# Two buffers for the rearranged and turned tiles of the sample compression, the bias table loaded behind the gathers, and more projection in the recurrence's first interval

## What is computed

```python
def compress(rows, pe, w1, w2):
    b, length = rows.shape[:2]
    n_chunks = length // CMP_STRIDE
    r = CMP_BLOCK // CMP_STRIDE
    n_cmp = n_chunks - r + 1
    ch = rows[:, :n_chunks * CMP_STRIDE].reshape(b, n_chunks, CMP_STRIDE, N_KV_HEADS, HEAD_DIM)
    blocks = jnp.concatenate([ch[:, i:i + n_cmp] for i in range(r)], axis=2)
    blocks = blocks + pe[:, None, :]
    flat = jnp.transpose(blocks, (0, 1, 3, 2, 4)).reshape(b, n_cmp, N_KV_HEADS, CMP_BLOCK * HEAD_DIM)
    return jax.nn.gelu(flat @ w1) @ w2

def layer_front(h, lw):
    z = rmsnorm(h, lw['attn_norm']) @ lw['w_in']
    ...
```

## Time and profile before

| | |
|---|---|
| median of 3 runs | 1233.44 us (1232.53 to 1235.86) |
| the profiled execution | 1235.16 us |
| its span | 1233.3 us |
| PE busy, share of the span | 93% |
| DVE, ACT, POOL | 41%, 33%, 34% |
| mean granted clock of PE | 0.961 |

### The profile page before, as it was taken

The page is one execution under the profiler, slowest core; times in us unless marked ns, Lnnn a source line. Parts: engine busy times, 40 slices in busy tenths (PEclk is TensorE's granted clock), DMA queues, the critical chain, the costliest instruction groups (busy, mean ns, idle before and its releaser), DMA issues.

```text
span 1233.3 us, 19665 instructions
## 1 busy us (share of the span) xinstructions
PE 1150.4 (93%) x8351; PEld 992.8 (80%) x8351; DVE 503.9 (41%) x939; ACT 403.1 (33%) x728; POOL 421.4 (34%) x247
## 2 busy tenths in 40 slices
PE   4998999979798999889799999999999999999996
PEld 4996888868444457455579999999999999999996
DVE  4848787666000001667547533323233230011354
ACT  5422332332332213557542224232322221222413
POOL 1266688583200003000204432343434344434230
PEclk9988999989789999889999999999999999999999
DMA  7434274542583107000518222222333322323311
GB/s 202 131 71 125 57 225 139 165 139 87 110 147 121 48 1 267 24 2 2 172 47 276 86 86 69 86 86 87 88 89 92 92 82 78 93 78 99 108 30 73
DMA packets 162803, 125.08 MB, mean 101 GB/s; under 512 B 20699, under 2 KB 151227, under 8 KB 161180
## 3 DMA queue, kind: packets, MB, share of 16 engines
q1 hardware_dynamic: 156956, 102.59, 30.3%
q0 software_dynamic: 3456, 16.78, 4.1%
q10 hardware_dynamic: 2304, 4.46, 0.9%
HBM read 112.27 MB, written 15.69 MB: 104 GB/s over the span
## 4 chain that ended last, share of the span: by engine, by line
PE 84%; DVE 6%; ACT 4%; issue 2%; DMA 1%; POOL 1%; SPq 1%; ACTq 0%; DVEq 0%; POOLq 0%
PE pair L1694 15%; PE pair L1696 15%; PE pair L1695 15%; PE pair L1906 9%; PE pair L1658 4%; PE pair L1660 4%; PE pair L1659 4%; PE pair L1701 2%; PE pair L2088 2%; DVE arena L1181 2%; PE pair L1876 1%; PE pair L2058 1%; PE pair L1865 1%; PE pair L1890 1%; PE pair L2068 1%
## 5 line engine op out<-in xcount | busy, mean ns | idle before, releaser
L708 POOL TENSOR_TENSOR ring_r<-ring,ring_r 128x1024 fp32r<-128x1024 f32 (+2 forms) x123 | 289.2, 2359 | 502.8 <-ACT ring_r L807 502.1
L1694 PE MATMUL pair<-zT_r,ring_r 128*128 128x272 f32 x928 | 270.6, 292 | 0.0
L1696 PE MATMUL pair<-zT_r,ring_r 128*128 128x272 f32 x928 | 268.6, 289 | 0.0
L1695 PE MATMUL pair<-uT_r,ring_r 128*128 128x272 f32 x832 | 239.5, 288 | 0.0
L1694 PEld LDWEIGHTS pair<-zT_r,ring_r 128*128 128x128 f32 x928 | 174.7, 188 | 0.4
L1696 PEld LDWEIGHTS pair<-zT_r,ring_r 128*128 128x128 f32 x928 | 174.6, 188 | 0.0
L807 ACT ACTIVATE ring_r<-ring 128x1024 fp32r<-128x1024 f32 (+2 forms) x123 | 124.8, 1031 | 122.4 <-PE pair L1696 94.3
L1695 PEld LDWEIGHTS pair<-uT_r,ring_r 128*128 128x128 f32 x832 | 156.9, 189 | 0.3
L1658 PE MATMUL pair<-arena_r,ring_r 128*128 128x272 f32 (+1 forms) x496 | 147.9, 298 | 7.8 <-ACT arena L881 6.9
L1694 PE MATMUL pair<-arena_r,ring_r 128*128 128x272 f32 x512 | 148.7, 290 | 0.9 <-issue 0.9
L1696 PE MATMUL pair<-arena_r,ring_r 128*128 128x272 f32 x512 | 148.2, 289 | 0.0
(11 more groups left out here) (299 smaller groups left out, 1642.8 us busy)
## 6 DMA issues: line engine op xcount, KB each, us to landing
ring<-in_w_in SPq DMA_DIRECT2D x26, 512.0 KB, 5.0
ring<-in_w_ffn_gate SPq DMA_DIRECT2D x22, 512.0 KB, 3.8
ring<-in_w_ffn_up SPq DMA_DIRECT2D x22, 512.0 KB, 3.8
ring<-in_w_ffn_down SPq DMA_DIRECT2D x16, 512.0 KB, 4.0
mg_spill<-arena ACTq DMA_DIRECT2D x16, 272.0 KB, 4.3
arena<-mg_spill SPq DMA_DIRECT2D x8, 544.0 KB, 8.3
arena<-in_cmp_w_v SPq DMA_DIRECT2D x4, 1024.0 KB, 6.0
ring<-in_w_o SPq DMA_DIRECT2D x8, 512.0 KB, 4.1
```

The source lines that it names most:

```text
L708: eng.tensor_tensor(ring_r[:, n % RING, 0:slab_size(n)], ring[:, n % RING, 0:slab_size(n)], hi, ALU.subtract).then_inc(S["slab_split"], 1)
L1694: eng.matmul(out, w_hi, x_hi(k)[:, cols], start=n == 0, stop=False)
L1695: eng.matmul(out, w_hi, x_lo(k)[:, cols], start=False, stop=False)
L1696: ins = eng.matmul(out, w_lo, x_hi(k)[:, cols], start=False, stop=n == len(steps) - 1)
```

## The change

Five things change; the arithmetic stays.

1. `fill` takes 36 steps in interval 0 and 25 or 26 in the others, instead of 26 or 27.
2. POOL's gather 0 moves from behind rotation 13 to behind rotation 11, and ACT's `raw_copy(0)` from g = 12 to g = 13. Splits 33 to 35 move from ahead of gather 2 to behind gather 3; ACT's copies for them (`high_after` of the last three groups) move from the projection's end to behind `raw_copy(2)`.
3. `raw2` and `XT` are there twice, the second pieces in the arena where the projection's and the recurrence's tiles have been; `glu_sig` moves to make room, and a memset on DVE that now lies over the second XT moves behind `cs_done`.
4. PE issues the turns of the next batch among the hidden matmuls of this one, one bank (4 transposes) after every 4 matmuls, and the second product of a batch after the first 4 matmuls of the next.
5. The bias table is loaded after the second half of the value network's `w1`, which gets a semaphore of its own, `w1_rest_in`.

```diff
-        XT = uT[:, :, :].rearrange("p a b -> p (a b)")[:, 0:4096].rearrange("p (q k n) -> p q k n", q=8, k=KV)
+        XT = [x.rearrange("p (q k n) -> p q k n", q=8, k=KV) for x in (uT[:, :, :].rearrange("p a b -> p (a b)")[:, 0:4096], ar(7304, 4096))]
-        raw2 = ar(22528, 2048)
+        raw2 = [ar(22528, 2048), ar(11528, 2048)]
...
             half_w1("cmp_w1_v", 0)
             eng.wait_ge(S["hid_done"], 8)
-            half_w1("cmp_w1_v", 1)
+            half_w1("cmp_w1_v", 1, "w1_rest_in")
+            for p0 in range(0, P, SHIFTS):
+                bias_table(p0)
...
-                if j in (13, 15):
-                    if j == 13:
+                if j in (11, 15):
+                    if j == 11:
                         eng.wait_ge(S["idx_ready"], 2)
                         eng.wait_ge(S["kv_out"], 16 * 12)
-                    gather_cmp(j // 2 - 6)
-            for n in range(33, 36):
-                split(n)
+                    gather_cmp(j // 15)
             for n in range(2, 8):
                 gather_cmp(n)
+                if n == 3:
+                    for m in range(33, 36):
+                        split(m)
...
             def raw_copy(n):
                 eng.wait_ge(S["raw_in"], 16 * (n + 1))
-                if n:
-                    eng.wait_ge(S["raw_turned"], 4 * n)
+                if n >= 2:
+                    eng.wait_ge(S["raw_turned"], 4 * (n - 1))
...
-                if g == 12:
+                if g == 13:
                     raw_copy(0)
...
-                high_after(name)
+                if g < 13:
+                    high_after(name)
...
+            for q in range(8):
+                if q == 4:
+                    raw_copy(1)
+                turn_out()
+            raw_copy(2)
+            for g in range(13, 2 * KC):
+                high_after(("mg%d" % (g % 2), g // 2))
+            raw_copy(3)
+            for batch in range(4):
+                if batch:
+                    second_out(batch - 1)
+                for q in range(8):
+                    if q == 6:
+                        hidden_out(batch, 0)
+                    if batch < 3:
+                        turn_out()
+                    if batch < 2 and q == 3:
+                        raw_copy(2 * batch + 4)
+                hidden_out(batch, 1)
+                if batch < 2:
+                    raw_copy(2 * batch + 5)
             second_out(3)
...
-            eng.memset(ce[:, :, CB_P:32], 0.0)
             eng.wait_ge(S["toep_in"], 16 * KV * P // SHIFTS)
             mx, sm = csum[:, 0:32], csum[:, 32:64]
             eng.wait_ge(S["cs_done"], 1)
+            eng.memset(ce[:, :, CB_P:32], 0.0)
...
-                fill(26 + j % 4 // 2)
+                fill(36 if j == 0 else 25 + j % 4 // 2)
...
             for batch in range(4):
-                for half in range(2):
-                    for h in range(2):
-                        hidden(h, half, batch)
-                if batch < 3:
-                    turns()
-                    turns()
-                second(batch // 2)
+                steps = hidden_steps(batch)
+                for q in range(8):
+                    for _ in itertools.islice(steps, 4):
+                        pass
+                    if q == 0 and batch:
+                        second((batch - 1) // 2, 4 + 2 * batch)
+                    if batch < 3:
+                        turn_rows()
+            second(1, 12)
```

More of the change, by code:

```diff
@@ L602, in _, with bias_table @@
             eng.wait_ge(S["line_out"], 16)
-            for p0 in range(0, P, SHIFTS):
+            def bias_table(p0):
                 for k in range(KV):
@@ L1894, in hidden @@
-            def hidden(h, half, batch):
-                nonlocal hid
-                if half == 0:
-                    if batch:
-                        eng.wait_ge(S["hid_taken"], 4 + 2 * (batch - 1) + h + 1)
-                    if h == 0:
-                        eng.wait_ge(S["turn_copied"], 8 * (batch + 1))
-                        eng.wait_ge(S["w1_in"], 64 if batch < 2 else 96)
-                out = bank(h)[:, 0:504].rearrange("p (k b c) -> p k b c", k=KV, c=CB_S)
-                for q in range(8):
-                    rhs = XT[:, q, :, :].rearrange("p k (b c) -> p k b c", c=64)[:, :, :, half:half + CB_S]
-                    ins = eng.matmul(out, w1[:, 8 * half + q, h * P:(h + 1) * P], rhs, start=half == 0 and q == 0, stop=half == 1 and q == 7)
-                if half:
-                    ins.then_inc(S["hid_done"], 1)
-                    hid += 1
-                elif h and batch == 1:
-                    ins.then_inc(S["half_done"], 1)
@@ L1913, in second @@
-            def second(kv):
+                n, q = turn // 4, turn % 4
+                ckv, ph = q // 2, q % 2
+                if q == 0:
+                    eng.wait_ge(S["raw_copied"], n + 1)
+                if turn >= 2:
+                    eng.wait_ge(S["turn_copied"], turn - 1)
+                for c in range(4):
+                    col = (4 * ph + c) * 256 + ckv * P
+                    ins = eng.transpose(bank(2 + turn % 2)[:, c * P:(c + 1) * P], raw2[n % 2][:, col:col + P], ident)
@@ new lines, in turn_rows, with hidden_steps @@
+                ins.then_inc(S["raw_turned"], 1)
+                turn += 1
+            def hidden_steps(batch):
+                for half in range(2):
+                    for h in range(2):
+                        if half == 0:
+                            if batch:
+                                eng.wait_ge(S["hid_taken"], 4 + 2 * (batch - 1) + h + 1)
+                            if h == 0:
+                                eng.wait_ge(S["turn_copied"], 8 * (batch + 1))
+                                eng.wait_ge(S["w1_in"], 64 if batch < 2 else 80)
+                        elif h == 0 and batch == 2:
+                            eng.wait_ge(S["w1_rest_in"], 16)
+                        out = bank(h)[:, 0:504].rearrange("p (k b c) -> p k b c", k=KV, c=CB_S)
+                        for q in range(8):
+                            rhs = XT[batch % 2][:, q, :, :].rearrange("p k (b c) -> p k b c", c=64)[:, :, :, half:half + CB_S]
+                            ins = eng.matmul(out, w1[:, 8 * half + q, h * P:(h + 1) * P], rhs, start=half == 0 and q == 0, stop=half == 1 and q == 7)
+                            if q == 7 and half:
+                                ins.then_inc(S["hid_done"], 1)
+                            elif q == 7 and h and batch == 1:
+                                ins.then_inc(S["half_done"], 1)
+                            yield q
```

67 lines of the change are left out of this document (24 added, 43 removed).

## The result

The changed kernel takes **1196.32 us** in the median of 4 runs (1193.35 to 1198.02) against 1233.9 beside it: a ratio of **0.969**, 95% interval 0.9671 to 0.9709. The profiled execution took 1197.42 us with a span of 1195.6. The forecast was 1202, its range 1196 to 1211: the direction and the mechanism held, the gain came out some 6 us larger than the 31.3 forecast.

> The changed kernel as it is, beside the next ones on the same chip: 1196 (1193 to 1199), 0.969 of before.

The account below looks back on a forecast made before the run. PE, busy 93% of the span, was taken as the bound, so time is won only where it waits or runs at lower clock. 8.3 + 8.0 + 7.1 + 8.0 − 0.1 = 31.3 off 1233.44 gave 1202 us, range 1196 to 1211.

Parts of the forecast that it names:

- Part 1: Recurrence, interval 0: 36 steps instead of 26 remove PE's wait on DVE and half clock at x_pair(2); net 8.3 us.
- Part 2: Recurrence, mg 12: earlier gather 0 and later raw_copy(0) remove PE's 6.9 us wait on ACT and half clock; net 8.0.
- Part 3: Projection's end to first hidden matmul: ACT's copies no longer stand behind late slab loads; 16.20 becomes 9.1, net 7.1 us.
- a case that I had given to a rival: Clock falls in small gaps left in part 3 and between batches, one to three times: 1205 to 1211 us; chance 0.13.
- Part 4: The four batches: turns among hidden matmuls and double buffers cut 139.5 us to 131.5; net 8.0.
- The rest: Bias table's move, w1_in split and glu_sig cost nothing; the memset moved behind cs_done costs 0.1 us.
- POOL bound one interval only: Rival in the recurrence: POOL's splits and DVE hold PE in each interval, half of parts 1 and 2 lost: 1210; chance 0.05.
- The buffers do not overlap: Rival in parts 3 and 4: every tile still waits for gather and copy, little won there: about 1217 us; chance 0.03.
- The rival on the slower side: Interleaved transposes hold PE at its lower clock through batches 0 to 2: 1297 us; chance 0.04.

Follow-up runs that it names:

- e2: The kernel before with only gather_cmp(0) two rotations earlier on POOL and raw_copy(0) at g = 13: 1231.85 us, ratio 0.9985.
- e5: The changed kernel with the bias table's 16 transfers back at their old place on SP's queue: 1210.4 us.
- e4: The changed kernel with a batch's eight turns in one piece behind its 32 hidden matmuls, both double buffers kept: 1206.24 us.
- e6: The changed kernel with every turn issued twice, or eight times, over the same bank: batches of 136.8 us and 199.7 us.
- e1: The kernel before with only the projection steps per interval changed (36, then 25 and 26 in turn): 1224.07 us, ratio 0.9918.

## Why the prediction's mechanism held, and which step of its sum failed

**Part 1** held: no wait at x_pair(2), no stretch at 0.50, x_pair(4) at 137.95 (forecast near 138), one new wait of 1.2 on POOL at slab 13 (forecast 1.0). **Part 2** held in kind and missed in two sizes. The new wait at x_pair(14) was 1.5, not 2.5 (DVE's recurrence 12 started at 241.93, 27.8 behind x_pair(10), where I had 28.2, and PE came a little later than I had it). And the half clock behind the old wait of 6.9 cost more than x_pair(14) and y_sums. PE, in order of time in the kernel before:

```profile
273.31 0.60 PE L1658 MATMUL pair<-arena_r,ring_r 128*128 128x272 f32 x1 [6.86 <-ACT arena L881]
273.71 0.43 PE L1659 MATMUL pair<-uT_r,ring_r 128*128 128x272 f32 x1
...
282.64 0.42 PE L1659 MATMUL pair<-uT_r,ring_r 128*128 128x272 f32 x1
282.87 0.32 PE L1660 MATMUL pair<-arena_r,ring_r 128*128 128x272 f32 x1
283.02 0.29 PE L1658 MATMUL pair<-arena_r,ring_r 128*128 128x272 f32 x1
```

The steps ahead of x_pair(14) and behind y_sums ran slow too, from 273.31 to 282.9: 9.6 us, a loss of 4.8 where I counted 3.6. With a wait of 0.6 on an earlier output of ACT that went away as well, the terms are 5.6 + 3.7 − 1.2 + 6.9 + 4.8 − 1.5 + 0.6 = 18.9, against 18.55 measured and 16.3 forecast. The prediction counted the six steps that part 1 brings into part 2's sum, but not that part 2 hangs on them: e2 shows that without them 4.47 of the 6.9 come back.

**Part 3** held: 9.5 against 9.1. ACT's last output ended when I had it, and the turns paced as forecast; the 2.6 us for raw_copy(1), which I had left in, let the clock fall there, a case that I had given to a rival.

**Part 4 is the step that was mis-sized.** The sum of terms was short by 37.7 − 0.7 − 31.3 = 5.7 us, of which 3.85 lie here, 2.25 in parts 1 and 2, and −0.4 in part 3. I made the work of 126.0 from row lengths, 27.31 for a batch, 0.52 for a turn, 4.3 for the second products, and put 0.02 on each of 48 switches. But a row runs on under the next one: a group of four matmuls advances PE by 3.38, so four batches by 108.2 (1.0 less), a turn by 0.437, so 24 by 10.5 (2.0 less), the second products by 4.0 (0.3 less), and a switch costs nothing (1.0 less). The boundaries came to 0.90 each, as forecast at 0.91; batch 0's waits to 0.3 and 0.6 for 1.1 and 0.6 (0.8 less). That makes 108.2 + 10.5 + 4.0 + 2.7 + 0.9 = 126.3; the other 1.3 up to 127.66 is the end of the last row and some 0.2 at each restart behind a wait or a second product, which I had not counted. The range's low end, 1196, took the switches and both new waits at nothing, but not this: it kept the row lengths.

**The rest** was right in its number and wrong in its reason. I gave the bias table's move nothing, by looking only at who wants the table. It is a condition of part 4: with turns inside the batches a raw tile has a half batch to arrive, and e5 shows 14 us lost if the table runs beside the gathers. The 5.9 us that part 4 took for a gather already assumed the move. DVE waits for no transfer between 300 and 560 us, as the prediction asked.

**The rivals.** The clock fell in one small place (part 3), not in the batches. POOL bound one interval only. "The buffers do not overlap" did not come: within the batches PE waits 0.3 for a raw copy and 0.6 for a bank's copy behind one. But e4 leaves 10.7 of the 11.85 us unwon without the new order, and e5 all of them with the table in its old place. The rival on the slower side is ruled out by e6.

## What to carry to other kernels

Cost work that is moved among other work by the distance from start to start of a row and the next, not by row lengths, which overlap; and count a slow stretch of the clock by its whole length in time, not by the instruction that stands out. Where a buffer shortens the time that a transfer has to land, look at what else the DMA engines carry in that time: a table moved out of the way can be worth more than the buffer. A second buffer may win most of its worth only with an order of work that spreads its consumer's small pieces among long ones: here 10.7 of the 11.85 us hang on that order, and all of them on the table's place.

## What the runs showed of the hardware

An indirect gather of 1 MB that lands in 5.9 us alone took 20.4 us beside sixteen plain transfers of 228 KB on another queue, at a DMA share of 1.05. Transposes that fill half of PE's time, and 14.1 us of fp32 transposes alone, left the granted clock at 1.00. Behind a wait of 7 us the lower clock lasted from 264.84 to between 269.09 and 269.65 in e1, where only projection steps followed, and 9.6 us in the kernel before, where x_pair(14) and its y_sums followed: the same wait had two prices. Why the two differ was not tried apart.
